# First feed-forward projection of a decoder layer: 20 of 32 column units computed as rows of 1024 columns, partly by Strassen, and transposed

## What is computed

```python
D_MODEL, SEQ, D_FF = 2048, 256, 8192
mix = jnp.concatenate([y_rwkv, y_diff], axis=-1) @ w_out[l]
x = _layer_norm(DEEPNORM_ALPHA * x + mix, ln1_gain[l], ln1_bias[l])
h = jnp.square(jax.nn.relu(x @ w_ff1[l])) @ w_ff2[l]      # x @ w_ff1 is what is changed
x = _layer_norm(DEEPNORM_ALPHA * x + h, ln2_gain[l], ln2_bias[l])
```

## Time and profile before

| | us |
|---|---|
| median of 3 runs | 1240.58 (1239.41 to 1242.42) |
| the profiled execution | 1239.0 |
| its span, first to last instruction | 1237.2 |
| mean granted TensorE clock | 0.997 of full speed |

### The profile page before, as it was taken

One profiled execution on the slowest core, in us unless ns is written; L12 is line 12 of the kernel. 1 busy time (PEld: TensorE's weight loads), 2 busy tenths in 40 slices (PEclk: granted clock), 3 DMA queues, 4 the chain that ended last, 5 costly groups with the idle time before them and its releaser, 6 DMA issues.

```text
span 1237.2 us, 22985 instructions
## 1 busy us (share of the span) xinstructions
PE 1219.4 (99%) x9585; PEld 1033.4 (84%) x9585; DVE 860.7 (70%) x909; ACT 619.4 (50%) x674; POOL 137.7 (11%) x94
## 2 busy tenths in 40 slices
PE   8999999999999999999999999999999999999997
PEld 8888888888779878888888888888888888888884
DVE  5688888475766375765554545555689998889987
ACT  5754455546566254453334343434455555565552
POOL 0022112000000000055000000000122221022220
PEclk9999999999999999999999999999999999999998
DMA  9454465332431156635555554545565555555541
GB/s 338 146 213 173 171 246 198 104 138 104 157 117 54 39 222 225 261 105 202 179 194 185 188 193 180 201 174 201 173 269 204 204 204 205 174 206 203 202 168 69
DMA packets 34206, 222.38 MB, mean 180 GB/s; under 512 B 4717, under 2 KB 5101, under 8 KB 8782
## 3 DMA queue, kind: packets, MB, share of 16 engines
q1 hardware_dynamic: 34126, 221.21, 50.0%
HBM read 219.10 MB, written 2.10 MB: 179 GB/s over the span
## 4 chain that ended last, share of the span: by engine, by line
PE 55%; DVE 1%; ACT 0%; issue 0%; DVEq 0%
PE ps L531 55%; DVE stats L2135 0%; DVE xres L2132 0%; DVE xres L2325 0%; DVE xres L2323 0%; DVE xres L2313 0%; ACT xres L1283 0%; DVE xres L2317 0%; DVE moments L2138 0%; PE ps L1175 0%; DVE moments L2145 0%; ACT moments L1283 0%; DVE shift_diag L2339 0%; DVE moments L2144 0%; DVEq L2125 0%
## 5 line engine op out<-in xcount | busy, mean ns | idle before, releaser
L1708 DVE TENSOR_TENSOR wlo<-stage,whi 128x2048 fp32r<-128x2048 f32 x166 | 387.0, 2331 | 244.5 <-ACT whi L1283 243.7
L531 PE MATMUL ps<-acts,whi 128*128 128x512 f32 (+1 forms) x1728 | 535.0, 392 | 3.2 <-DVE wlo L1735 1.9
L1283 ACT ACTIVATE whi<-stage 128x2048 fp32r<-128x2048 f32 (+2 forms) x196 | 361.8, 1847 | 303.0 <-PE ps L531 297.4
L531 PEld LDWEIGHTS ps<-acts,wlo 128*128 128x128 f32 x1680 | 316.1, 188 | 72.1
L531 PE MATMUL ps<-acts,wlo 128*128 128x256 f32 x1680 | 334.9, 278 | 0.0
L531 PEld LDWEIGHTS ps<-acts,whi 128*128 128x128 f32 x1728 | 264.4, 189 | 7.7 <-DVE wlo L1735 2.1
L531 PE MATMUL ps<-whi,shi 128*128 128x512 f32 x402 | 110.8, 389 | 0.0
L531 PE MATMUL ps<-wlo,shi 128*128 128x512 f32 x402 | 110.8, 389 | 0.0
L531 PE MATMUL ps<-whi,slo 128*128 128x512 f32 x402 | 110.8, 389 | 0.0
L1283 ACT ACTIVATE shi<-hid 128x512 fp32r<-128x512 f32 x64 | 40.5, 633 | 127.9 <-PE ps L531 127.9
L531 PEld LDWEIGHTS ps<-wlo,shi 128*128 128x128 f32 x402 | 75.5, 188 | 15.7
(11 more groups left out here) (290 smaller groups left out, 1394.5 us busy)
## 6 DMA issues: line engine op xcount, KB each, us to landing
stage<-w_ff SPq DMA_DIRECT2D x128, 1024.0 KB, 4.8
stage<-w_in SPq DMA_DIRECT2D x48, 1024.0 KB, 4.9
stage<-w_out SPq DMA_DIRECT2D x16, 1024.0 KB, 4.8
stage<-w_in SPq DMA_DIRECT2D x6, 512.0 KB, 9.4
xstage<-xT SPq DMA_DIRECT2D x4, 512.0 KB, 7.5
TM_TT<-eyes SPq DMA_DIRECT2D x4, 512.0 KB, 7.5
xres<-x SPq DMA_DIRECT2D x1, 2048.0 KB, 9.4
gain<-ln_gain SPq DMA_DIRECT2D x2, 1024.0 KB, 7.7
```

Of the source, the lines that this page charges most:

```text
L531: return pe.matmul(out, lhsT, rhs, start=start, stop=stop, skip_group_check=True)
L1283: return act.activation(out, in_, func, **kw)
L1708: TTn(wlo[k0 % NHL][:, :], stage[k0 % NST][:, :], f(whi[k0 % NHL][:, :]), ALU.subtract).then_inc(s_lo, 1)
```

## The change

Units 0 to 3 (8 slabs) and 24 to 31 (16 slabs) stay as they were. The 40 slabs between, now called row slabs 0 to 39, become 5 groups of 1024 columns; `layout` arranges their weights so that a slab holds two blocks k of 1024 columns. In a group of 8 slabs, slabs 0, 1, 3, 5 and 7 are plain (`row_slab`) and slabs 2, 4 and 6 are done by Strassen's products (`row_quad`). The activations stand still, so a group's result has the tokens on the partitions. VectorE adds the shared products (`row_shared_taken`, four instructions) and then the direct ones (`rows_added`, four) into `rsum`; TensorE turns `rsum` by 16 transposes of 128x128 into the banks of the group (`rows_turned`), in the middle of the next group's first slab, and for the last group in the middle of row slab 41, the second slab after the rows; ScalarE copies with ReLU and squares in place (`rows_kept`). The sums of activations `xsum` are the same for all groups: GpSimd forms them once, nine instructions after its last `gained`; ScalarE rounds them (`xshi`) and VectorE takes the remainders (`xslo`). `rsum` also holds the sums of weights, rounded to `rthi`, with the remainder `rtlo`. Some semaphores at the kernel's start are merged, and counts that later stages wait for are shifted. The core of the diff:

```diff
+ROW_GROUPS, ROW_QUADS = 5, (2, 4, 6)
+N_ROWQ = ROW_GROUPS * len(ROW_QUADS)
+N_UNITS = N_FF1 - 4 * ROW_GROUPS
+G_ROWS, G_LATE = G_FF1 + 8, G_FF1 + 8 * ROW_GROUPS
...
+            def rows_turned(r):
+                for i, (a, q) in enumerate(((0, 0), (0, 1), (1, 0), (1, 1))):
+                    pe.wait_ge(s_radd, 4 * r + i + 1)
+                    for b in range(4):
+                        last = pe.transpose(ps[:, direct_bank(r % 2, a, q), P * b:P * b + P],
+                                            rsum[:, i, P * b:P * b + P], ID)
+                    last.then_inc(s_ft, 1)
+            def row_slab(s):
+                g, r, j = G_ROWS + s, s // 8, s % 8
+                w, h = g % NHL, r % 2
+                pe.wait_ge(s_hi, g + 1)
+                for kk, part in ((0, 0), (0, 1), (0, 2), (1, 0), (1, 1), (1, 2)):
+                    if (kk, part) == (0, 2):
+                        pe.wait_ge(s_lo, g + 1)
+                    if (kk, part) == (1, 0) and r and j == 0:
+                        rows_turned(r - 1)
+                    still, moving = ((acthi, whi), (actlo, whi), (acthi, wlo))[part]
+                    for a, q in ((0, 0), (0, 1), (1, 0), (1, 1)):
+                        cols = slice(HALF * kk + 512 * q, HALF * kk + 512 * q + 512)
+                        last = mm(ps[:, direct_bank(h, a, q), :], still[:, 2 * j + kk, tok(a)], moving[w][:, cols],
+                                  start=(j == 0 and kk == 0 and part == 0), stop=(j == 7 and kk == 1 and part == 2))
+                last.then_inc(s_used, 1)
...
+            def row_quad(s):
...
+                own = ((shared[0], plain[0, 0], whole[1], 0), (direct[0, 0], plain[0, 1], whole[2], None),
+                       (direct[0, 1], summed[3], whole[3], None))
+                mixed = ((direct[1, 0], plain[1, 1], added[3], None), (shared[1], summed[1], added[0], 1),
+                         (shared[2], summed[0], added[1], 2), (shared[3], summed[2], added[2], 3))
+                pe.wait_ge(s_hi, g + 1)
+                pe.wait_ge(s_ql, len(ROW_QUADS))
+                for part in range(2):
+                    for acc, x, y, m in own:
+                        mm(acc, x[part], y[0], start=first and m is not None and part == 0, stop=False)
+                pe.wait_ge(s_qh, row_rounded(s))
+                for part in range(2):
+                    for acc, x, y, m in mixed:
+                        mm(acc, x[part], y[0], start=first and m is not None and part == 0, stop=False)
+                pe.wait_ge(s_ql, len(ROW_QUADS) + k + 1)
+                for acc, x, y, m in mixed:
+                    mm(acc, x[0], y[1], start=False, stop=end and m is not None)
+                pe.wait_ge(s_lo, g + 1)
+                for acc, x, y, m in own:
+                    last = mm(acc, x[0], y[1], start=False, stop=end and m is not None)
+                last.then_inc(s_used, 1)
...
+            for s in range(8 * ROW_GROUPS):
+                r, j = s // 8, s % 8
+                if j == 0:
+                    if r:
+                        pe.wait_ge(s_pd, 4 * r)
+                    else:
+                        pe.wait_ge(s_sum, 3)
+                if j == ROW_QUADS[0]:
+                    if r:
+                        pe.wait_ge(s_rkept, 5 * r - 1)
+                    else:
+                        pe.wait_ge(s_sum, 4)
+                if is_row_quad(s):
+                    row_quad(s)
+                else:
+                    row_slab(s)
+            pe.wait_ge(s_pd, PD0)
+            for k in range(2):
+                pairs(late_bank(k), G_LATE + 8 + 2 * k, G_LATE + 8 + 2 * k,
+                      between=None if k else lambda: rows_turned(ROW_GROUPS - 1))
...
+            def rows_kept(r):
+                for i, (a, q) in enumerate(((0, 0), (0, 1), (1, 0), (1, 1))):
+                    act.wait_ge(s_ft, 4 * r + i + 2)
+                    A(hid[:, 8 + 8 * r + 4 * q:12 + 8 * r + 4 * q, tok(a)],
+                      ps[:, direct_bank(r % 2, a, q), :].rearrange("p (b t) -> p b t", b=4), ACT.Relu).then_inc(s_rkept, 1)
+                act.wait_ge(s_rkept, 5 * r + 4)
+                x = hid[:, 8 + 8 * r:16 + 8 * r, :]
+                A(x, x, ACT.Square).then_inc(s_rkept, 1)
+            for c in range(len(ROW_QUADS)):
+                act.wait_ge(s_pl, 2 * NB + 3 * c + 3)
+                A(xshi[c][:, :, :], xsum[:, c, :, :], ACT.Copy).then_inc(s_qh, 1)
+            for s in range(1, 8 * ROW_GROUPS + 2):
+                r, j = s // 8, s % 8
+                if j == 0:
+                    row_shared_copied(r - 1)
+                if is_row_quad(s):
+                    hi_own(G_ROWS + s)
+                elif s > 1:
+                    hi(G_ROWS + s, G_ROWS + s)
+                if j == 1 and r:
+                    rows_kept(r - 1)
+                if is_row_quad(s + 1):
+                    row_sums_hi(s + 1)
...
+            def row_sums(s):
+                g, k, r = G_ROWS + s, row_quad_no(s), s // 8
+                src = stage[g % NST][:, :].rearrange("p (j q) -> p j q", j=4)
+                if s % 8 == ROW_QUADS[0]:
+                    dve.wait_ge(s_ft, 4 * r + 1)
+                dve.wait_ge(s_ql, len(ROW_QUADS) + k)
+                dve.wait_ge(s_stage[g % NST], 16 * (g // NST + 1))
+                TTn(rsum[:, 0:2, :], src[:, 1::2, :], src[:, 0:1, :].broadcast_to([P, 2, 512]), ALU.add).then_inc(s_qs, 1)
+                dve.wait_ge(s_qs, 3 * k + 1)
+                TTn(rsum[:, 2, :], rsum[:, 0, :], src[:, 3, :], ALU.add).then_inc(s_qs, 1)
+                dve.wait_ge(s_qs, 3 * k + 2)
+                TTn(rsum[:, 3, :], rsum[:, 2, :], src[:, 2, :], ALU.add).then_inc(s_qs, 1)
...
+            for c in range(len(ROW_QUADS)):
+                dve.wait_ge(s_qh, c + 1)
+                TTn(xslo[c][:, :, :], xsum[:, c, :, :], f(xshi[c][:, :, :]), ALU.subtract).then_inc(s_ql, 1)
+            for s in range(8 * ROW_GROUPS + 2):
+                r, j = s // 8, s % 8
+                if is_row_quad(s):
+                    row_sums_lo(s)
+                    lo_own(G_ROWS + s)
+                elif s > 1:
+                    lo(G_ROWS + s, G_ROWS + s)
+                if j == 0 and r:
+                    rows_added(r - 1)
+                if is_row_quad(s + 2):
+                    row_sums(s + 2)
+                if j == 7:
+                    row_shared_taken(r)
...
+            for c, j in enumerate(ROW_QUADS):
+                done = 2 * NB + 3 * c
+                x = x1f[:, 2 * j:2 * j + 2, :].rearrange("p k (a q) -> p (k a) q", a=TT_)
+                if c == 0:
+                    pool.wait_ge(s_lnp, 8)
+                PT(xsum[:, c, 0:2, :], x[:, 1:2, :].broadcast_to([P, 2, P]), x[:, 0::3, :], ALU.subtract).then_inc(s_pl, 1)
+                pool.wait_ge(s_pl, done + 1)
+                PT(xsum[:, c, 2, :], x[:, 0, :], xsum[:, c, 1, :], ALU.subtract).then_inc(s_pl, 1)
+                pool.wait_ge(s_pl, done + 2)
+                PT(xsum[:, c, 3, :], x[:, 2, :], xsum[:, c, 2, :], ALU.subtract).then_inc(s_pl, 1)
```

208 lines of the change are left out of this document (145 added, 63 removed).

## The result

The changed kernel takes 1252.91 us (median of 5 runs, 1252.49 to 1255.84) against 1240.12 us for the kernel before (5 runs beside them), a ratio of 1.0108 with a 95% interval of 1.0091 to 1.0124. The prediction was 1253.1 us, slower.

What follows compares the result with a forecast made beforehand. TensorE, 99% busy, was taken as the bound. -15.6 + 8.8 + 8.1 + 2.6 + 2.6 + 0.4 + 4.3 + 1.3 = +12.5 us on the median 1240.58 gave 1253.1 us, range 1247 to 1258.5.

Steps and rivals of the forecast that it cites:

- slabs: The 40 row slabs become 25 plain at 5.44 us and 15 Strassen at 4.76, from 5.575 each: -15.6 us.
- turning: 80 added 128x128 transposes on TensorE, 0.11 us each: +8.8 us.
- first wait: TensorE waits at slab 2, the first Strassen slab, for operands behind GpSimd's late xsum: +8.1 us.
- its clock: TensorE's clock halves after a long idle: +2.6 us behind the first wait, +1.3 behind the wait at slab 42.
- group waits: In groups 2 to 5, TensorE waits 0.65 us for VectorE's slab 1 remainder, queued behind slab 2's sums: +2.6 us.
- slab 40: At the end of the rows, its remainder stands behind VectorE's four steps on the shared products: +0.4 us.
- slab 42: Its rounding stands behind ScalarE's five steps on the last group's result, so TensorE waits: +4.3 us.
- layout's 5.4 us: Part of the gain on the row slabs: 24 wide matmuls for 32, 40 x 0.135 us.
- second rival: GpSimd held up in full, 3.44 us per triple of xsum additions, wait 11.8: +16.2, 1256.8 us; chance 0.15.
- first rival: Both long idles occur but the clock stays full: +9.5, 1250.1 us; chance 0.17.
- rival on the other side: Faster: xsum done by 575.9, no wait at slab 2; +2.7, or -2.9 (1237.7 us) without slab 42's delay; chance 0.04.
- tail of 7.6 us: Chain from GpSimd's last xsum addition to TensorE's start of slab 2, 584.0 to 591.6.

Runs made afterwards that it cites:

- e7: Changed kernel without Strassen in the five groups: all eight slabs of each group plain, no operand sums or shared banks; 1251.65 us, ratio 1.0087.
- e5: Changed kernel with 60 of the 80 turning transposes left out, so that part of the result is missing; 1250.08 us, ratio 1.0072.
- e6: Changed kernel with 34 extra unread 512-column products on TensorE during its wait at slab 2; 1254.26 us, ratio 1.0108.
- e4_all_four: Changed kernel reordered: GpSimd's sums first, slab 2's own rounding first, slab 42's before output copies, later groups' slab 1 remainder before sums; 1241.74 us, ratio 1.0012.
- e3: Changed kernel with ScalarE rounding slab 42's weights before its share of the last group's output copies; 1250.50 us, ratio 1.0089.
- e1: Changed kernel with GpSimd's nine xsum additions before its gains and biases, and another buffer for xsum; 1251.85 us, ratio 1.0096.
- f1_order: e4_all_four with operand sums' rounding and remainders one unit earlier, and slab 3's remainder before slab 4's weight sums; 1241.49 us, ratio 1.0014.

## Why the prediction was right, term by term

| term | forecast | measured | from |
|---|---|---|---|
| slabs | -15.6 | -15.6 | e7: 5.44 a plain slab; plain and Strassen pair 10.2 |
| turning | +8.8 | +8.9 | 5 x 1.79 (e7), 0.109 each (e5) |
| first wait | +8.1 | +8.2 | timeline |
| its clock | +2.6 | +2.8 | slab 2 took 7.58 us for 4.76; 2.7 by e6 |
| group waits | +2.6 | +2.8 | B of e4_all_four |
| slab 40 | +0.4 | +0.6 | timeline, 0.41 + 0.16 |
| slab 42 | +4.3 | +4.4 | timeline, 4.22 + 0.16 |
| its clock | +1.3 | +1.7 | C of e3, 6.04 less 4.38 |
| sum | +12.5 | +13.8 | the stage itself: 366.84 - 352.94 = 13.9 |

**The slabs and the turning.** The pair of a plain and a Strassen slab: the products of two Strassen slabs that follow each other start 10.2 us apart in the changed kernel (693.07 and 703.27), 5.44 + 4.76, so the mixed sources cost nothing. The layout's 5.4 us came as the rows said. The Trainium skill, "TensorE: Matmul & The Clock Gate", section "Wait — 56ns, not 53.3ns?", gives a fixed 2.5 ns or so a matmul, by which the layout would be worth near nothing: with 0.02 us saved a slab, the estimate for e7 is turnings 8 x 5.555 + 1.8 = 46.2 us apart. They stand 45.3 us apart, and the measurement decides.

**The chain to slab 2.** GpSimd finished its last bias at 575.7 (forecast 575.3), was held until VectorE's remainder of 575.21 had ended and came out of its first addition at 578.5; the three triples with their remainders were 2.25 us apart (2.2), the last xsum ended at 584.55 (584.0), TensorE started at 592.11 (591.6) and wanted to at 583.9 (583.5). All links are late by the same 0.4 to 0.5 us, since the stage itself began 0.4 us later. The second rival, GpSimd held up in full, did not come: only the first addition met a long VectorE instruction with two SBUF tiles, and the middle one of each triple a short one (0.93 to 0.97 us, where e1 has 0.46 at 546.77). The Trainium skill, "SBUF — State Buffer", section "Who interferes with whom", names the pair that collides, a VectorE instruction with two SBUF inputs and a GpSimd one that reads SBUF, and frees one with at most one SBUF input outside its two-port modes; the trace agrees with the first part (the first xsum addition took 2.67 us, the one of the same shape 0.74 at 580.01), and f1_order shows the same collision from VectorE's side.

**The clock.** At slab 2 it fell as at the kernel's end, and TensorE worked 5.8 us at half speed against 5.2 there. The first rival (clock unmoved) is out, and e6 shows the size. That wait and clock came within 0.2 us of the forecast is partly luck: with the same code up to there, e3's trace has 7.4 and 1.8 us (slab 2 took 6.53 for 4.76), e5's 8.2 and 2.1. At slab 42 I had halved the price because I could not tell whether it would fall; it did, and 1.7 us against 1.3 is the largest miss of a term.

**The waits of order.** Group waits, slab 40 and slab 42 were read from the order of the instructions and VectorE's and ScalarE's durations. e4_all_four removed the group waits and e3_late_order that of slab 42 with nothing but order, and 2.8 and 6.0 us came back. No experiment took aim at slab 40; its wait of 0.41 stands in all of them but e7, which has no shared products.

**What made the total closer than its parts.** The terms were 1.4 us short in sum. The profiled span grew by 13.5 us, since the start lies 0.4 us later and the tail from ashi on is 336.39 us against 337.17; the medians grew by 12.8. The tail is 336.2 to 337.3 in all traces, the kernel before's second one (336.21) included, so that is variation between runs and no effect of the change. The prediction of 1253.1 for 1252.9 is in part luck of this size; right by its reasons it is to about 1.5 us.

**Where a reason failed.** The prediction's rival on the other side said that no wait arises at slab 2 if xsum ends by 575.9. In e1_early_sums xsum ended at 547.8 and 4.1 us of wait were left. The step that failed is the tail of 7.6 us hung onto GpSimd's last addition: it took VectorE as free for the remainders and sums, and VectorE had its remainder of slab 1, which GpSimd slows (3.27 us from 578.24), and an output to do until 582.8. GpSimd's chain and VectorE's queue both ended late, and the second stood hidden behind the first. It didn't touch the forecast, since that chain was the later one, but it made the faster case look nearer than it was, and it is why the expectations of e1_early_sums and e4_all_four were too good by 3.7 and 4 to 5 us.

## What to carry to other kernels

A saving in matmuls on a bound TensorE is worth its full size only while the engines that prepare operands stay ahead; here 10.2 us of saved products turned into 3.2 us of loss, because a new chain of small sums ran through three engines and met, in each, work that was queued ahead of it. Walk such a chain at its **first** use, where nothing has been prepared ahead, and look at each engine's queue at every new step; the order alone (and another buffer for one small tensor) was worth 16.8 us of stage here (366.84 to 350.04). When a wait can't be avoided, try to put matmuls into its middle: the single idle at slab 2 cost the clock as well, 11.0 us in all, and about the same idle in five pieces 9.1. Compare kernels by a stage between two fixed instructions when a change of 0.2% is at stake, and look at what the stage does in a second trace: here it repeated exactly before the change, and by 1.5 us in part A behind it.
